# First half's output weights by gated rows and its output product in three split passes

## The reference

```python
y = rms(y * silu(z)) * ssd_norm_w            # z = xn @ w_z, per group of 512 channels
y_ssd = y @ w_ssd_out                        # 2048 -> 1024
o = rms(o) * gla_norm_w * silu(g)            # per head of 256 channels
y_gla = o @ w_gla_out                        # 1024 -> 1024
gate_ssd, gate_gla = split(sigmoid(merge))   # merge = xn @ w_merge, 2 x 1024
x = x + (gate_ssd * y_ssd + gate_gla * y_gla) @ w_out
hn = rmsnorm(x, norm2_w)
x = x + peer(hn)   # 8 heads: queries, two top-16 lists of 128 keys, 16 experts (rows of 2 x 1024) per head
```

## Time and profile before

| | |
|---|---|
| median of 3 runs | 2376.61 us (2373.93 to 2379.61) |
| the profiled execution | 2376.9 us, span 2375.1 us |
| mean granted TensorE clock | 0.956 |
| busy over the span | TensorE 85%, weight loads 52%, VectorE 66%, ScalarE 29%, Pool 28% |

### The profile page before, as it was taken

The page is one execution under the profiler, slowest core; times in us unless marked ns, Lnnn a source line. Parts: engine busy times, 40 slices in busy tenths (PEclk is TensorE's granted clock), DMA queues, the critical chain, the costliest instruction groups (busy, mean ns, idle before and its releaser), DMA issues.

```text
span 2375.1 us, 23408 instructions
## 1 busy us (share of the span) xinstructions
PE 2018.4 (85%) x7474; PEld 1240.1 (52%) x7490; DVE 1578.5 (66%) x3589; ACT 687.9 (29%) x1722; POOL 665.6 (28%) x628
## 2 busy tenths in 40 slices
PE   7888999999998799989899898598777777777776
PEld 5555555789846566665544686275222323223231
DVE  4666543562125799997775998897767677576764
ACT  4333221441112444433334211122322222122222
POOL 0222133000002323233322343334443434334341
PEclk9999999999999999999999999799899999899999
DMA  6233522544459999999999999999999999999996
GB/s 249 95 142 127 188 103 104 176 139 146 156 176 350 349 338 337 344 366 413 367 367 341 388 415 416 417 409 413 420 420 420 418 415 420 365 408 409 421 408 279
DMA packets 152781, 750.32 MB, mean 316 GB/s; under 512 B 21225, under 2 KB 47401, under 8 KB 83922
## 3 DMA queue, kind: packets, MB, share of 16 engines
q0 software_dynamic: 74880, 545.29, 57.2%
q1 hardware_dynamic: 77778, 203.53, 23.6%
HBM read 717.62 MB, written 31.07 MB: 315 GB/s over the span
## 4 chain that ended last, share of the span: by engine, by line
PE 35%; DMA 25%; DVE 15%; issue 4%; ACT 2%; POOL 0%; DVEq 0%; SPq 0%; POOLq 0%; ACTq 0%
DMA t_rows<-in_experts,t_idx 21%; PE bank L2856 9%; PE bank L2525 7%; PE bank L2781 6%; DVE t_rows L2468 5%; PE bank L2556 3%; DVE t_fin L2487 2%; PE bank L2793 2%; PE bank L2527 2%; DMA wring<-in_w_merge 2%; PE bank L2528 1%; PE bank L2529 1%; DVE t_mixed L2270 1%; PE bank L2669 1%; DMA wring<-in_w_gla 1%
## 5 line engine op out<-in xcount | busy, mean ns | idle before, releaser
L1950 POOL DMA_INDIRECT t_rows<-in_experts,t_idx x520 | 577.3, 1110 | 1355.5 <-PE bank L2856 746.6
L2856 PE MATMUL bank<-t_rows,t_diag 128*128 128x512 f32 (+1 forms) x1528 | 743.7, 634 | 215.5 <-ACT t_diag L2190 215.2
L2468 DVE CUSTOM_DVE_ANT_0 t_rows<-t_rows,t_hn_cur 128x1024 f32<-128x1024 f32 x520 | 632.3, 1220 | 221.8 <-DMA t_rows<-in_experts,t_idx 219.9
L2856 PEld LDWEIGHTS bank<-t_rows,t_diag 128*128 128x128 f32 (+1 forms) x1528 | 290.4, 198 | 638.1 <-issue 323.8
L2190 ACT ACTIVATE t_diag<-ident,t_gg 128x128 f32<-128x128 f32 x374 | 131.0, 395 | 432.9 <-DVE t_gg L2475 432.9
L2525 PE MATMUL bank<-t_xs,wring 128*128 128x256 f32 x1024 | 235.9, 389 | 9.3 <-ACT t_last L1975 4.9
L2525 PEld LDWEIGHTS bank<-t_xs,wring 128*128 128x128 f32 x1024 | 198.6, 196 | 47.1 <-issue 18.3
L2487 DVE SCALAR_TENSOR_TENSOR t_fin<-t_rows,t_gg,t_fin 128x1024 f32<-128x1024 f32 x138 | 177.3, 1285 | 10.7
L2781 PE MATMUL bank<-t_yoT,wring 128*128 128x264 f32 (+1 forms) x768 | 173.9, 385 | 5.0 <-DMA wring<-in_w_merge 2.7
L2177 ACT ACTIVATE t_gel<-t_hid 128x2 f32<-128x2 f32 x260 | 53.0, 204 | 420.5 <-DVE t_hid L2468 419.6
L2781 PEld LDWEIGHTS bank<-t_yoT,wring 128*128 128x128 f32 x768 | 144.4, 190 | 31.1 <-DMA wring<-in_w_merge 7.8
(11 more groups left out here) (430 smaller groups left out, 2542.0 us busy)
## 6 DMA issues: line engine op xcount, KB each, us to landing
wring<-in_w_merge SPq DMA_DIRECT2D x80, 512.0 KB, 6.7
wring<-in_w_z SPq DMA_DIRECT2D x32, 512.0 KB, 6.3
wring<-in_w_query SPq DMA_DIRECT2D x32, 512.0 KB, 9.2
ring<-in_w_ssd SPq DMA_DIRECT2D x4, 3072.0 KB, 12.1
wring<-in_w_ssd SPq DMA_DIRECT2D x24, 512.0 KB, 7.6
t_rows<-in_experts,t_idx POOLq DMA_INDIRECT x520, 14.6
s_sst<-in_state_ssd SPq DMA_DIRECT2D x4, 2048.0 KB, 7.8
o_sssd<-s_sst SPq DMA_DIRECT2D x16, 512.0 KB, 2.6
```

The source lines that it names most:

```text
L1950: nc.gpsimd.indirect_dma_start(rows[:, n % RING, :], None, k.dram["experts"], bass.IndirectOffsetOnAxis(idx[:, u, s:s + 1], 0)).then_inc(r ...
L2468: nc.vector.tensor_tensor_reduce(out=v, in0=v, in1=hn_cur[:, r % 2, :], scale=1.0, scalar=0.0, op0=ALU.mult, op1=ALU.add, accum_out=hid[:, ...
L2856: last = nc.tensor.matmul(ps[bank][0:round_rows(r), :], diag[:, d % DIAGS, 0:round_rows(r)], rows[:, n % RING, D + half * 512:D + half * 5 ...
```

## The change

- The units `my`, `mo` and `ou` of the first half are marked split, so 32 more units are cast and subtracted.
- `whl` gets a fourth slot (`SLOTS_LO` = 4, the tile `whl_last`). Cast and sub run four units ahead in place of three; those of unit 3 stand at the start of the tail. Before an `oc` task, held casts are written out too.
- `yoT` is split into `yhi` (task `yhi`, ScalarE copy) and `ylo` (`ylo`, VectorE subtraction), one task per scale. `my` waits for the low parts it reads, `mo` of j = 0 too. The roots move from the first to the third unit of a slab, the scales to other units.
- `mixT` is split into the two halves of `xhl` (`mhi`, `mlo`): tiles 0 to 6 after the last gate unit (`xhl` is free from there), tile 7 after the last mix.
- `ou` and `oc` go through `row_products`: three passes with the rows' parts as the stationary operand and the weights' parts as the moving one. The first `ou` unit waits for the splits of two tiles and no longer for the last mix.
- The order of j = 0 and 1: mg(0), mg(1), my(0), my(1), mo(0), mo(1). `sig` of j = 0 moves ahead of mg(1), the first `my` behind the last transposition.

The core of the diff (left out: declarations of semaphores and slices, the allocation of `yhi`, `ylo` and `whl_last`):

```diff
-    for j in range(KD):
+    for j in range(2):
         for i in range(2):
-            if j != 1:
-                units.add(("mg", p, j, i), True)
+            units.add(("mg", p, j, i), True)
+    for j in range(2):
         for u in range(2):
-            if (j, u) != (1, 0):
-                units.add(("my", p, j, u), False)
-        if j == 0:
-            for i in range(2):
-                units.add(("mg", p, 1, i), True)
-            units.add(("my", p, 1, 0), False)
-        units.add(("mo", p, j), False)
+            units.add(("my", p, j, u), True)
+    for j in range(2):
+        units.add(("mo", p, j), True)
+    for j in range(2, KD):
+        for i in range(2):
+            units.add(("mg", p, j, i), True)
+        for u in range(2):
+            units.add(("my", p, j, u), True)
+        units.add(("mo", p, j), True)
     for i in range(2):
         for u in range(4):
-            units.add(("ou", p, i, u), False)
+            units.add(("ou", p, i, u), True)
...
+    put(0, "cast", SPLITS)
+    put(0, "sub", SPLITS)
...
             if s < 6:
                 use("zu", s, u)
-            elif u < 2:
-                use("mg", p, 0, u)
             else:
-                use("my", p, 0, u - 2)
+                use("mg", p, u // 2, u % 2)
...
-                if t == 2:
-                    put(0, "root", 0)
-                if t == 4:
-                    put(0, "root", 1)
-                if t == 5:
-                    put(0, "root", 2)
             if s == 6 and u == 3:
                 put(0, "scale", 4)
+                put(0, "yhi", 4)
                 put(0, "scale", 5)
-                put(0, "sig", p, 0)
+                put(0, "yhi", 5)
...
+            if u == 2 and t in (2, 4, 5):
+                put(0, "root", t // 2 - 1 + t % 2)
             put(.7, "tr", t, u)
             for kind in (("mul", "sq") if t < 4 else ("sq", "mul")):
                 put(0, kind, t, u)
-            if t in (2, 4) and u in (1, 3):
-                put(0, "scale", t - 2 + u // 2)
+            if t in (2, 4) and u == 3:
+                put(0, "scale", t - 2)
+            if t in (3, 5):
+                if u == 1:
+                    put(0, "scale", t - 2)
+                put(0, "yhi" if u in (0, 2) else "ylo", t - 3 + u // 2)
+            if t == 5 and u == 1:
+                put(0, "sig", p, 0)
...
     put(.5, "ss", 5, 3)
     put(0, "ms", 7)
     put(0, "root", 3)
+    use("my", p, 0, 0)
+    for h in range(2):
+        put(0, "ylo", 4 + h)
     for h in range(2, 4):
         put(0, "scale", 4 + h)
+        put(0, "yhi", 4 + h)
+    for h in range(2, 4):
+        put(0, "ylo", 4 + h)
     for j in range(KD):
         if j > 1:
             use("mg", p, j, 0)
             use("mg", p, j, 1)
+        if j == KD - 1:
+            for i in range(j):
+                put(0, "mhi", i)
+                put(0, "mlo", i)
         if j == 0:
-            use("mg", p, 1, 0)
-            use("mg", p, 1, 1)
+            use("my", p, 0, 1)
             use("my", p, 1, 0)
-        if j:
+            use("my", p, 1, 1)
+        else:
             put(0, "sig", p, j)
-            if j > 1:
-                use("my", p, j, 0)
+        if j > 1:
+            use("my", p, j, 0)
             use("my", p, j, 1)
         use("mo", p, j)
         put(0, "mix", p, j)
+    put(0, "mhi", KD - 1)
+    put(0, "mlo", KD - 1)
...
-        if n + SPLITS < len(units.names) and units.split[n + SPLITS]:
-            held = [(0, ("cast", n + SPLITS)), (0, ("sub", n + SPLITS))]
+        if n + SLOTS_LO < len(units.names) and units.split[n + SLOTS_LO]:
+            held = [(0, ("cast", n + SLOTS_LO)), (0, ("sub", n + SLOTS_LO))]
...
+                elif kind == "yhi":
+                    i = at[0]
+                    act.wait_ge(scale_done, i + 1)
+                    nc.scalar.copy(yhi[:, scaled(i), :], yoT[:, scaled(i), :]).then_inc(y_hi, 1)
+                elif kind == "mhi":
+                    j = at[0]
+                    act.wait_ge(unit_used, MG_LAST)
+                    act.wait_ge(mix_done, N[("mix", 0, j)])
+                    nc.scalar.copy(xhl[:, 0, j, :], mixT[:, j, :]).then_inc(m_hi, 1)
...
+            def row_products(bank, n, c, kt):
+
+                out, cols = ps[bank][0:part_rows(c), :], slice(kt % 2 * 512, (kt % 2 + 1) * 512)
+                first, final = kt == 0, kt == KD - 1
+                if not units.split[n]:
+                    return nc.tensor.matmul(out, mixT[:, kt, part_cols(c)], wring[:, n % WR, cols], start=first, stop=final)
+                hi, lo = whl[split_no[n] % SLOTS_LO][:, 0, cols], whl[split_no[n] % SLOTS_LO][:, 1, cols]
+                nc.tensor.matmul(out, xhl[:, 0, kt, part_cols(c)], hi, start=first, stop=False)
+                nc.tensor.matmul(out, xhl[:, 0, kt, part_cols(c)], lo, start=False, stop=False)
+                return nc.tensor.matmul(out, xhl[:, 1, kt, part_cols(c)], hi, start=False, stop=final)
...
                     if p == 0 and kind == "my":
-                        pe.wait_ge(scale_done, 4)
+                        pe.wait_ge(y_lo, 2 * at[2] + 2)
...
                         if kind == "mo" and p == 0 and j == 0 and kt % 2 == 0:
-                            pe.wait_ge(scale_done, 5 + kt // 2)
-                        last = nc.tensor.matmul(ps[bank][:, 0:width(p)], wring[:, n % WR, kt * P:(kt + 1) * P], yoT[:, at_k + kt, 0:width(p)],
-                                                start=kt == 0 and at_k in (0, 2 * KD), stop=kt == KD - 1 and at_k != 0)
+                            pe.wait_ge(y_lo, 5 + kt // 2)
+                        last = products(bank, n, slice(kt * P, (kt + 1) * P), yoT, at_k + kt, width(p), kt == 0 and at_k in (0, 2 * KD),
+                                        kt == KD - 1 and at_k != 0, (yhi, ylo))
...
-                    pe.wait_ge(w_here[n % WR], 16 * (n // WR + 1))
-                    pe.wait_ge(mix_done, N[("mix", p, KD - 1)])
+                    weights(n)
                     pe.wait_ge(sig_done, N[("sig", p, KD - 1)])
+                    if p == 0:
+                        pe.wait_ge(m_lo, 2 * u + 2)
+                    else:
+                        pe.wait_ge(mix_done, N[("mix", p, KD - 1)])
                     for c in range(2 if (p, i) == (0, 1) else 0, parts_of(p)):
+                        if c == 2 and i == 0 and u == 0:
+                            pe.wait_ge(mix_done, N[("mix", p, KD - 1)])
                         for kk in range(2):
-                            kt = 2 * u + kk
-                            last = nc.tensor.matmul(ps[2 + 3 * i + c][0:part_rows(c), :], mixT[:, kt, part_cols(c)], wring[:, n % WR, kk * 512:(kk + 1) * 512],
-                                                    start=kt == 0, stop=kt == KD - 1)
+                            last = row_products(2 + 3 * i + c, n, c, 2 * u + kk)
```

47 lines of the change are left out of this document (31 added, 16 removed).

## The result

Beside each other, the changed kernel took 2353.15 us (four runs, 2348.66 to 2354.06) and the kernel before 2376.32 (four runs, 2373.93 to 2379.61): ratio 0.9898, 95% interval 0.988 to 0.9915. On a second occasion it was 0.9945 (0.9929 to 0.9962). That the span lost about as much as the stretch described next (22.8) is in part luck: the stretch began 2.03 us later than before, and what follows it was 2.15 us shorter. In the profile the gain sits in one stretch, from the first product of the tail stage to the first query product, and that stretch is the measure in most of what follows.

A forecast was written before the change was run, and what follows sets the result against it. TensorE was taken to bound the stretch before the queries, its shift carried 1:1 to the end. Terms -1.0 - 4.0 + 8.0 + 1.6 - 11.9 - 1.0 - 10.1 = -18.4 from 2376.9 gave 2358.5 us; range 2349 to 2369.

The forecast's parts named there:

- The output product: Last product before the queries: 144 split passes at 0.226 us replace 42.7 us of f32, -10.1 us (bounds -11.3 and -8.9).
- The rival of cheap columns: Output product: 512 columns cost no more than 264, 0.121 us a pass, 15 us more gain, 2343 us; chance 0.02.
- the one of weight loads that do not hide: Output product: a 0.19 us weight load stands before each pass, 17.2 us more than before, 2386 us; chance 0.06.
- The start of the tail: Start of the tail stage: the fourth split is cast at once, not behind the first product, -1.0 us.
- The moved gates: First gates to the o products: four waits of TensorE, 8.6 us less the 0.54 there before, +8.0 us.
- A: Second gate product waits for the first sigmoid, whose banks it uses: 2.7 us, not below 2.0.
- B: Wait at the sum of squares: the last square stands behind two splits on ScalarE, 3.0 us against 0.54 before.
- D: Second o product waits for the first mix, since both o products use one bank: 2.1 us, not below 1.2.
- The clock: First gates: one of the added waits causes a stretch at half the granted clock, +1.6 us (bounds 0 and 4.8).
- Six units at j = 0 and 1: First two output channels: six weight units in three split passes in place of f32, 0.66 us saved each, -4.0 us.
- The rival that the tail gives a part back: Tail behind the first query product: its gathers give the gain back, 2376 us; chance 0.05.
- shorter waits: First gates and output product: two waits vanish, no clock loss, output pass at its lower bound, 2352 us; chance 0.12.

The follow-up runs named there:

- experiment 9: Changed kernel with 138 of the output product's 144 passes of 512 columns each cut into two of 256; first pass to first query product 37.35 us, 0.38 more.
- Experiment 4: Changed kernel with the order repaired at three waits of TensorE (second gates, last square, second o product): 2353.87 us, 0.9932 of the kernel before, stretch 249.48 us.
- experiments 5 and 6: Changed kernel with one repair each: a y product between the gates (stretch 254.70 and 252.66 us); casts of tiles 4 and 5 behind the last square (251.93 us).
- experiments 2: Changed kernel with only the output product back in f32: 2361.44 us, 0.9954 of the kernel before, stretch 262.22 us.
- the one with the small load: Changed kernel with one second-half weight load cut from 512 KB to 8 KB: median 2350.60 us, 0.9908 of the kernel before with the same cut.
- moved gates in f32: Changed kernel with none of the added units split, so all their products are f32: 2384.10 us, 1.0057 of the kernel before, stretch 281.00 us.
- before, with the small load: Kernel before with one second-half weight load cut from 512 KB to 8 KB: median 2372.34 us, 0.9987 of the kernel before.

## Why the prediction came out as it did

The forecast was -18.4 us and 2358.5; the profiled execution took 2354.06 and the stretch lost 22.8. The path was right: the gain arises where TensorE is alone in the chain, and the waits that pay for it stand where they were put. By steps:

- **The loop**, -11.9: 640.10 - 553.10 = 87.0, 14.50 a period against 16.49: -11.9. Right, with no wait for VectorE.
- **The output product**, -10.1: from 640.10 to the 120th pass at 667.70 it is 0.232 us each, 33.4 for all 144 in place of 42.7: -9.3. The mechanism was right and the size within its bounds, but 0.226 took something off for a fixed part paid once per pass (and 144 x 0.226 is 32.5, not 32.6). There is next to none: 0.121 / 264 is 0.458 ns a column, 0.232 / 512 is 0.453, and experiment 9 puts at most 3 ns on an extra pass. The upper bound, columns times the price of a column, was the value to take. The rival of cheap columns and the one of weight loads that do not hide are both refuted. Where the Trainium skill ("TensorE: Matmul & The Clock Gate") gives 131 ns for 512 columns in a stream (section "Back-to-back issue gap") and lets a weight load overlap only with another row group (Part 3, section "The mechanism"), this trace differs from both for these fp32r passes: 0.232 us a pass, with a load of 0.188 us ahead of each 128-row pass that adds nothing.
- **The wait for the last mix**, -1.0: gone. The first pass begins at 640.10, 0.12 behind the start of the last gated pass. From the end of the loop to the first query product the stretch lost 10.7 us where these two terms were forecast at 11.1.
- **The start of the tail**, -1.0: the fourth unit begins 2.34 us into the stage in place of 3.43. Up to the first gate product the stretch gained 0.70 only; in between TensorE now waits 1.20 us for a gate of the last z slab, which takes a part back; "nothing, bound +2" held, at a part of its bound.
- **The moved gates**, +8.0: the waits are 1.96, 2.36, 0.21 and 1.46, 5.99, less the 0.54 that was there: +5.45. All four are where the prediction put them, with the releasers it named, and each was counted 0.6 to 0.7 too long, so they stay under the 7 to 10 us that I named, and A at 1.96 just below the 2.0 under which it could not fall. For A the trace shows the term: 0.7 stood for the rest of a table load, and none stands between the last square and the two activations; it comes later, at 523.52 (see the lines below). For B to D no single term was found. Experiment 4 prices three of them at 3.2 to 3.7 us in the stretch. As a price they are not independent: most of A's and two thirds of B's repair is kept, the rest moves to the next wait of the same queues (experiments 5 and 6).

```profile
520.85 0.39 ACT L2139 ACTIVATE t_sq<-bank 128x264 f32<-128x264 f32 x1 [1.62 <-PE bank L2785]
521.90 0.67 ACT L2155 ACTIVATE t_mixed<-bank 128x264 f32<-128x264 f32 x2 [0.66 <-DVE t_yoT L2438]
...
523.52 1.28 ACT L2144 ACT_TABLE_LOAD   x1
```

- **The clock**, +1.6: in this pair of profiles it is -1.7, since the fall behind the first gate product was in the profile of before and in none of the changed kernel's two. This is the term that was most in error, 3.3 us. It was read as a property of the order ("one of A, B and D causes a stretch more"); it differs from one execution of the same order to the next. Over the executions that have the changed order untouched up to j = 2 (the two profiles of the changed kernel, experiments 2, 9 and the one with the small load) it fell 4 times behind 15 waits of 1.68 to 2.36 us, 0.8 an execution or some 1.3 us; in the order before it fell in two of three, some 1.1 us an execution. On the mean the term is near nothing.
- **Six units at j = 0 and 1**, -4.0: with +5.45 and -1.7 this makes -0.25 from the first gate product to the start of j = 2 (553.10), where the change is +0.54 (39.70 to 40.24). The difference lies in the six units: from 533.32 to 553.10, less the waits of 0.21 and 1.46, they take 18.1 us and not 6 x 2.90 = 17.4. The passes beside a wait are dearer, since a wait is counted from the end of a record of 0.28 us where otherwise the next pass begins after 0.12, and the first records behind a wait are 0.36 to 0.48 long. So the saving is 3.3.
- **The tail**, 1:1: its length changed by -2.15 us, under the 3 that I named. But two executions of the same changed kernel differ by 12, so that test could not have shown much. The better evidence is the tails without the wait for that load: 1675.1 (changed), 1674.8 (moved gates in f32), 1676.0 (repair of B), 1676.7 (half the columns) and 1674.3 (before, with the small load), with first query products from 672.37 to 700.22. A start 28 us later ends 27 us later, so in executions without the wait nothing is given back. With a wait of 6.6 to 6.7 us the tails scatter by more: 1687.2, 1684.1, 1680.5 and 1682.8 for first query products at 677.76, 677.80, 683.51 and 697.50. Whether the earlier start makes the wait longer is not shown: it averages 3.4 us in the three profiles of the order before and 2.9 in the eleven with moved gates, but on the second occasion all four versions were 3.5 to 11 us slower beside the kernel before than their stretches say, and the kernel before was not profiled there. The rival that the tail gives a part back stays open to that extent.

That the stretch lost 4.4 us more than forecast is therefore five terms: the clock -3.3, the waits -2.6, the six units +0.7, the output product with its wait for the mix +0.4 and the start +0.3. The sum came nearer than its parts, since they err both ways. The rival "shorter waits" named the clock and the waits, with the output pass at its opposite bound.

## What to carry to other kernels

A TensorE pass of split operands is priced by its columns from the nearest stretch of passes, and a wait that follows from two queues in strict order can be worked out to 0.6 to 0.7 us here, but repairing one hands a part of it to the next. A rare stretch of low clock in a profile is to be averaged over several executions before it is booked to either side. Where whole executions scatter by ten microseconds and the change is worth twenty, the stretch between two fixed events of the profile is the measure, and the rest of the span is examined for its own chance. An edit that is to remove one wait is checked in the trace first: the load that it makes small has to be the one whose landing ends the wait.

## What was not expected of the hardware

The granted clock fell from 1.00 (2.4 GHz) to 0.50 (1.2 GHz) behind the same wait in some executions and not in others: in 5 of 14 profiles behind the 1.68 us ahead of the first gate product, in 1 of 8 behind 1.96 us, 1 of 6 behind 2.35 to 2.36, both times behind 2.84 and the one time behind 3.65; never behind the eight waits D of 1.08 to 1.48, and in none of the 14 behind the 1.89 to 1.90 us ahead of the first product of the tail stage. Each fall cost 1.6 to 1.7 us, and 2.7 behind the longest wait. What decides between two executions of one kernel no run here shows.

One weight load of 512 KB, issued beside the gathers (DMA share 1.02 and 405 GB/s from 1117 to 1123 us in the changed kernel), lands 7.6 to 22.1 us after its issue, and with it goes up to 11 us of the first round: in 14 profiles the round is 532.6 to 535.0 us where TensorE does not wait for it, 535.3 and 535.9 with 0.57 and 2.56 us, 537.2 to 542.3 with 3.5 to 4.6, and 540.6 to 543.4 with 6.6 to 6.7. What decides when it lands no run here shows.
